# A hybrid decoder layer on one core: the mixer's units and attention heads put in another order, with roots, splits and constants done in other places

## What is computed

```
xn = rmsnorm(x, g_mix);  proj = xn @ w_in
q, k, v, u_pool, q_mem, gate_logits = split(proj)
q, k = rotary(rmsnorm(q, q_norm)), rotary(rmsnorm(k, k_norm))        # 8 heads, 2 maps of 64 each
o = (softmax(q1 k1) - lam * softmax(q2 k2)) @ v                      # causal, per head
y_attn = (rmsnorm(o, g_subln) * 0.8) @ w_b_attn
y_pool = multiscale_pool(u_pool) @ w_b_pool
y_mem  = softmax(rmsnorm(q_mem) rmsnorm(km) / sqrt(128)) @ vm @ w_b_mem   # km, vm = rmsnorm(mem) @ w_mem_kv
h = x + (g0*y_attn + g1*y_pool + g2*y_mem) @ w_out                   # g = sigmoid(gate_logits + b_gates)
out = h + moe(rmsnorm(h, g_ffn))                                     # top 4 of 32 experts, clamped SwiGLU
```

## Time and profile before

| | |
|---|---|
| median of 3 runs | 1288.76 us |
| the profiled execution, its own time | 1286.68 us |
| its span in the profile | 1284.8 us |
| granted TensorE clock, mean share of 2.4 GHz | 0.983 |
| TensorE busy | 1175.9 us, 92% of the span |
| VectorE busy | 464.6 us, 36% |
| ScalarE busy | 251.3 us, 20% |
| GpSimd busy | 20.8 us, 2% |
| DMA | 458.50 MB, mean 357 GB/s |

### The profile page before, as it was taken

The page is one execution under the profiler, slowest core; times in us unless marked ns, Lnnn a source line. Parts: engine busy times, 40 slices in busy tenths (PEclk is TensorE's granted clock), DMA queues, the critical chain, the costliest instruction groups (busy, mean ns, idle before and its releaser), DMA issues.

```text
span 1284.8 us, 13949 instructions
## 1 busy us (share of the span) xinstructions
PE 1175.9 (92%) x5444; PEld 590.3 (46%) x5444; DVE 464.6 (36%) x814; ACT 251.3 (20%) x378; POOL 20.8 (2%) x29
## 2 busy tenths in 40 slices
PE   6898999997889999999999999999999999999997
PEld 5686787775743343434344343434434333333332
DVE  6679878875441222122122222222121212212131
ACT  5444555542010010001001010100100010001100
POOL 0200000010000000000000000000000000000000
PEclk8998999998989999999999999999999999999999
DMA  8544355476679999999999999999999999999996
GB/s 284 204 133 162 131 206 173 146 264 251 245 293 425 396 389 430 427 429 428 429 428 429 428 429 428 429 428 429 428 429 428 429 428 428 428 428 428 428 428 287
DMA packets 59480, 458.50 MB, mean 357 GB/s; under 512 B 9216, under 2 KB 9856, under 8 KB 34880
## 3 DMA queue, kind: packets, MB, share of 16 engines
q1 hardware_dynamic: 57168, 454.18, 85.8%
q0 software_dynamic: 1104, 3.93, 0.9%
q10 hardware_dynamic: 1184, 0.07, 0.1%
HBM read 457.11 MB, written 1.05 MB: 357 GB/s over the span
## 4 chain that ended last, share of the span: by engine, by line
PE 68%; DMA 16%; DVE 10%; ACT 3%; issue 2%; DVEq 0%; ACTq 0%; SPq 0%
PE bank L1495 29%; DMA experts_ring<-in_w_down 14%; PE bank L1547 14%; PE bank L1253 12%; PE bank L1515 5%; PE bank L1483 3%; DVE ring_split L774 3%; PE bank L1501 2%; ACT region L744 1%; PE bank L1502 1%; PE bank L1222 1%; DMA small<-in_g_mix 1%; DMA ring<-in_w_in 1%; DVE region L1173 1%; ACT prob L649 1%
## 5 line engine op out<-in xcount | busy, mean ns | idle before, releaser
L1495 PE MATMUL bank<-experts_ring,region 128*64 128x512 f32 x2048 | 454.0, 596 | 11.5 <-DVE region L1182 6.6
L1495 PEld LDWEIGHTS bank<-experts_ring,region 128*64 128x64 f32 x2048 | 145.2, 137 | 291.6 <-issue 286.3
L1547 PE MATMUL bank<-experts_ring,region 128*64 128x512 f32 x1024 | 229.0, 596 | 31.8 <-ACT region L744 25.0
L1253 PE MATMUL bank<-ring_split,region_split 128*128 128x512 f32 x768 | 234.5, 407 | 21.2 <-DVE ring_split L774 11.3
L1253 PEld LDWEIGHTS bank<-ring_split,region_split 128*128 128x128 f32 x768 | 147.2, 195 | 56.0 <-DVE ring_split L774 13.0
L1547 PEld LDWEIGHTS bank<-experts_ring,region 128*64 128x64 f32 x1024 | 73.1, 137 | 167.1 <-issue 125.5
L1253 PE MATMUL bank<-ring_split 128*128 128x512 f32 x288 | 114.8, 399 | 0.0
L1207 DVE COPY region<-bank 64x512 f32<-64x512 f32 x32 | 22.2, 694 | 237.1 <-PE bank L1547 237.1
L1190 DVE TENSOR_SCALAR region<-bank 128x512 f32<-128x512 f32 x32 | 22.1, 692 | 209.7 <-PE bank L1502 209.7
L774 DVE TENSOR_TENSOR ring_split<-ring,ring_split 128x2048 fp32r<-128x2048 f32 x42 | 95.8, 2288 | 0.3
L529 ACT ACTIVATE ring_split<-ring 128x2048 fp32r<-128x2048 f32 x42 | 79.9, 1910 | 39.8 <-DMA ring<-in_w_out 16.8
(11 more groups left out here) (167 smaller groups left out, 616.3 us busy)
## 6 DMA issues: line engine op xcount, KB each, us to landing
experts_ring<-in_w_gate SPq DMA_DIRECT2D x64, 2048.0 KB, 26.2
experts_ring<-in_w_up SPq DMA_DIRECT2D x64, 2048.0 KB, 25.3
experts_ring<-in_w_down SPq DMA_DIRECT2D x64, 2048.0 KB, 28.2
ring<-in_w_in SPq DMA_DIRECT2D x28, 1024.0 KB, 5.2
ring<-in_w_mem_kv SPq DMA_DIRECT2D x4, 1024.0 KB, 8.9
ring<-in_w_b_attn SPq DMA_DIRECT2D x4, 1024.0 KB, 5.1
ring<-in_w_out SPq DMA_DIRECT2D x4, 1024.0 KB, 5.1
region<-in_b_gates POOLq DMA_DIRECT2D x6, 512.0 KB, 4.9
```

The source lines that it names most:

```text
L1253: ins = nc.tensor.matmul(UB[u % 3][:, :], a[:, k, toks], b[:, cols], start=(k == 0 and m == 0), stop=(k == k_n - 1 and m == 2))
L1495: ins = nc.tensor.matmul(dst[h * SLOTS:(h + 1) * SLOTS, :], XE[:, kk, e * SLOTS:(e + 1) * SLOTS], w[:, k, h * HALF:(h + 1) * HALF], start= ...
L1547: ins = nc.tensor.matmul(bank[2][h * SLOTS:(h + 1) * SLOTS, :], AHT[:, k, half * SLOTS:(half + 1) * SLOTS], w[:, k, h * HALF:(h + 1) * HAL ...
```

## The change

The order of the pieces becomes `pool, mk, q0, mv, q1, qm, k0, v0, k1, v1`, so that the q and k pieces, which are rotated, alternate with others. Piece 0 is multiplied as plain float32 from the raw halves, 8 matmuls a unit, with no split of halves 0 and 1. The mean square becomes a sum whose 1/n sits in the Square's scale, and every root is an addition and a power on GpSimd, `inverse_root`; ScalarE's square roots and VectorE's reciprocals are gone. The norms of q (attention) and q_mem are not applied to the rows: they go into the scale of the exponentials and into the factor of the maxima. Each head's output is squared, scaled, turned and split by itself (`o_squares`, `o_out`, `turn_o`, `oT`, `oT_lower`), inside the head loop. One table `SPLIT_AT` replaces the two: ScalarE and VectorE both do half 2n+3 with piece n's first unit and half 2n+4 with its second. The short vectors come packed, in three DMAs. The head loop's pass h now holds units 21+2h and 22+2h, and the copy of turned merged blocks no longer stands behind four upper halves.

```diff
-PIECES = ["pool", "mk", "mv", "qm", "q0", "q1", "k0", "k1", "v0", "v1", "gp0", "gp1", "wbp",
+PIECES = ["pool", "mk", "q0", "mv", "q1", "qm", "k0", "v0", "k1", "v1", "gp0", "gp1", "wbp",
...
-    for _at, _u, _H in ((UPPER_AT, _first, 2 * _n + 4), (UPPER_AT, _second, 2 * _n + 5),
-                        (LOWER_AT, _first, 2 * _n + 3), (LOWER_AT, _second, 2 * _n + 4)):
+    for _u, _H in ((_first, 2 * _n + 3), (_second, 2 * _n + 4)):
         if _H < 2 * len(PIECES):
-            _at[_u] = _H
+            SPLIT_AT[_u] = _H
...
+            def inverse_root(cols, eps, signal):
+
+                n_eps[0] += 1
+                nc.gpsimd.tensor_scalar(cols, cols, eps, None, ALU.add).then_inc(eps_added, 1)
+                pool.wait_ge(eps_added, n_eps[0])
+                nc.gpsimd.tensor_tensor(cols, cols, minus_half.to_broadcast([P, cols.shape[1]]), ALU.pow).then_inc(signal, 1)
...
+            def o_root(h):
+                pool.wait_ge(o_squared, 2 * h + 2)
+                inverse_root(stat[:, 128 + 2 * h:130 + 2 * h], EPS, o_scale_ready)
...
             for h in range(HEADS):
-                for_gate = [u for u in (22 + 2 * h, 23 + 2 * h) if UNITS[u][1][0] == "g"]
+                a, b = 21 + 2 * h, 22 + 2 * h
+                if h:
+                    o_squares(h - 1)
                 if h + 1 < HEADS:
                     exps(h + 1)
-                if h == HEADS - 1:
-                    aT(h)
-                if 22 + 2 * h in for_gate:
-                    gate_exp(22 + 2 * h)
-                if h < HEADS - 1:
-                    aT(h)
-                hi_at(22 + 2 * h)
+                if h:
+                    o_out(h - 1)
+                aT(h)
+                gate_exp_of(a)
                 if h + 2 < HEADS:
                     qkT(h + 2)
...
+                hi_after(a)
+                if h:
+                    oT(h - 1)
+                gate_exp_of(b)
+                hi_after(b)
...
-                group_root(u - 6, slice(col, col + 8), HD)
-                link(nc.vector.tensor_tensor(a, raw, stat[:, col:col + 8].unsqueeze(2).to_broadcast([P, 8, HD]), ALU.mult))
...
+                if w == 0:
+                    nc.vector.tensor_tensor(raw, a, b, ALU.add).then_inc(normed, 1)
+                else:
+                    link(nc.vector.tensor_tensor(raw, a, b, ALU.add))
+                    normed_by(u, raw, HD, 8, normed)
...
             for h in range(HEADS):
                 if h + 1 < HEADS:
                     head_max(h + 1)
-                unit(22 + 2 * h)
+                unit(21 + 2 * h)
                 if h + 1 < HEADS:
                     head_weights(h + 1)
-                    unit(23 + 2 * h)
...
+                if h:
+                    oT_lower(h - 1)
+                unit(22 + 2 * h)
             unit(37)
+            oT_lower(HEADS - 1)
...
+                    if H < EARLY:
+                        if k % 4 == 0:
+                            pe.wait_ge(raw_in[H], 16)
+                            pe.wait_ge(xT_copied, 2 * t + k // 4 + 1)
+                        ins = nc.tensor.matmul(UB[u % 3][:, :], XNT[2][:, k, toks], raw(H)[:, cols], start=(k == 0), stop=(k == k_n - 1))
...
             def values(h):
                 pe.wait_ge(at_copied, h + 1)
                 if h >= 1:
-                    pe.wait_ge(o_copied, h)
+                    pe.wait_ge(o_copied, 2 * h)
+                    pe.wait_ge(oT_split, h)
...
+                if h:
+                    turn_o(h - 1)
+                unit(22 + 2 * h)
+                values(h)
+            unit(37)
+            turn_o(HEADS - 1)
             unit(38)
             unit(39)
-            for j in range(4):
-                t, h = divmod(j, 2)
-                pe.wait_ge(o_normed, t + 1)
-                turn4(bank[3 + j], [O[:, t, (4 * h + b) * P:(4 * h + b + 1) * P] for b in range(4)], oT_done)
-            pe.wait_ge(oT_split, 2)
+            pe.wait_ge(oT_split, HEADS)
             unit(40)
```

More of the change, by code:

```diff
@@ L491, in _ @@
             gate_bias(2, "a", 0)
+            for h in range(3, HEADS):
+                o_root(h)
             pool.wait_ge(pv_done, HEADS)
-            root(2, slice(128, 144))
             nc.gpsimd.memset(OE, 0.0).then_inc(seed_clear, 1)
@@ L503, in _ @@
             pool.dma_start(WR, w_router.rearrange("(k p) e -> p k e", p=P)).then_inc(late_in, 16)
-            root(3, slice(4, 5))
-            root(4, slice(5, 6))
+            for t in range(NT):
+                pool.wait_ge(squares, 5 + t)
+                inverse_root(stat[:, 4 + t:5 + t], EPS, h_inv)
         @block.scalar
@@ L700, in _ @@
-            for u in range(40, 44):
-                hi_at(u)
-            for j in range(4):
+                hi_after(a)
[3 more added lines that the diff above has]
+                hi_after(b)
+            o_squares(HEADS - 1)
+            o_out(HEADS - 1)
+            gate_exp(37)
+            hi_after(37)
+            oT(HEADS - 1)
+            for u in (38, 39):
+                gate_exp(u)
+                hi_after(u)
+            hi_after(40)
+            hi_after(41)
@@ L820, in _ @@
+            dve.wait_ge(gain_in, 16)
+            for j in range(4):
+                x_turned(j)
+            lo_whole(2)
+            mem_turned(0)
+            mem_turned(1)
+            lo_after(0)
+            mem_turned(2)
+            mem_turned(3)
+            dve.wait_ge(unit_done, 2)
+            for j in range(4):
+                x_lower(j)
+            lo_after(1)
+            dve.wait_ge(vec_in, 16 * 2)
             lam4 = tmp[:, 1, 0:4 * HD].rearrange("p (a n) -> p a n", a=4)
@@ L1275, in _ @@
             pe.wait_ge(mT_copied, 4)
-            for u in range(3, 8):
-                unit(u)
+            unit(3)
+            pe.wait_ge(xT_split, 4)
+            unit(4)
+            unit(5)
+            pe.wait_ge(bank_read[1], 1)
             pe.wait_ge(band_in, 32)
@@ L1351, in turn_qk @@
                     pe.wait_ge(qkT_copied, h)
[L1352 removed]
+                turn4(bank[3], [part(t, h // 4)[:, (h % 4) * P:(h % 4 + 1) * P] for part in (q_part, k_part) for t in range(NT)], qk_done)
             def scores(h):
@@ L1566 @@
     arrays, args = {}, []
-    for name in _INS + ["table", "band"]:
-        a = {"table": table, "band": band}.get(name)
+    for name in _INS + ["table", "band", "vectors"]:
+        a = {"table": table, "band": band, "vectors": short_vectors(inputs)}.get(name)
         a = np.ascontiguousarray(inputs[name]) if a is None else a
```

635 lines of the change are left out of this document (327 added, 308 removed).

## The result

The changed kernel takes 1306.67 us (median of four runs, 1305.25 to 1307.64). The kernel before, timed beside it, takes 1289.01 us, so the ratio is 1.014, with a 95% interval from 1.0126 to 1.0154: **17.7 us slower**. The forecast was 12.7 us slower. The profiled execution of the changed kernel took 1307.0 us, 20.3 more than the 1286.68 of the one before.

A forecast was written before the change was run, and what follows sets the result against it. Bound up to the turn of h: TensorE's units, with VectorE and ScalarE between. The walk's +5.7, plus 4.0 for clock and 3.0 for GpSimd, gave +12.7: 1299.4 us profiled, 1301.5 median; range 1291.5 to 1310.5.

The forecast's parts named there:

- terms for the clock: Lower TensorE clock: 2.0 us behind the memory branch's wait, 2.0 in the short passes; bounds 0 and 8 together.
- Mark 1: First units, up to the end of unit 3: 37.3 us against 45.5 before, a gain of 8.2.
- Mark 2: End of unit 19 at 148.2 us, including a 5.9 us TensorE wait after unit 14, behind unit 13's rotation.
- The walk: Stepping through the engines' new order with profile prices up to the turn of h: +5.7 us before three extra costs.
- GpSimd term: Roots on GpSimd slowed by VectorE's rotations: 0.75 us for each of four k units, 3.0; bounds 0 and 8.
- rival that GpSimd is shut out during rotations: Roots get nothing while VectorE rotates: +5 on the forecast, 1306.5 us; chance 0.15.
- Mark 3: Heads, from unit 19 to the end of unit 39: 152.1 us, ending at 300.3 against 272.5 before.
- full pass: Head-loop pass with two halves to split: 18.2 us, where TensorE needs about 13.5.
- the circle: Head loop: ScalarE and VectorE handle the same half, so neither works while the other does; 18.2 us a turn.
- short pass: Head-loop pass whose second unit is short, with one half to split: 13.9 us, where TensorE needs 8 to 11.
- Mark 4: Units 40 to 46, starting where unit 39 ends: 41.3 us, ending at 341.6 against 335.2 before.
- faster: Rival: heads stay at TensorE's pace and the gap behind unit 39 goes, 1259.4 us; chance 0.05.

The follow-up runs named there:

- run 2: The kernel before with ScalarE's upper half no longer one half ahead from unit 20 on: 1308.51 us, ratio 1.016.
- run 1: The changed kernel with ScalarE's upper half again one half ahead from unit 20 on: 1273.02 us, ratio 0.9887.
- experiment 6: The changed kernel with 8 transposes of the identity before each head's turning and values, from head 1 on: 1305.28 us, ratio 1.0133.
- experiments 3 and 4: Changed kernel with scores ahead of values: 1298.88 us; with the turned output's upper copy first: 1310.16, and its lower half ahead of the weights too: 1299.39.
- experiment 8: Changed kernel with upper halves' lead from unit 14 and memory maxima ahead of unit 13's rotation: 1266.72 us; last version, scores ahead of values too: 1259.39.

## Why the prediction was right, and where its sizes were off

The sign, the place and the mechanism were right. The marks, in us from the start. The forecast's include its terms for the clock and GpSimd where they fall (5.0 up to unit 19, 2.0 in the heads):

```
                      before   forecast   measured
end of unit 3          45.5      37.3       36.0
end of unit 19           -      153.2      149.7
end of unit 39        272.5     307.3      314.7
turn of h             335.2     348.6      356.3
```

*Mark 1* was 1.3 too dear. The loads of the first weights landed sooner than in the kernel before: half 2's upper half starts at 16.64, not at 18.26, and all that follows hangs on it.

*Mark 2.* The walk without extras gave 148.2, and 149.66 came, 1.5 more; with mark 1's gain of 1.3 that makes 2.8 to account for. Its parts hold: the first maximum was forecast for 104.7 and came at 103.22, and the wait of TensorE was 5.9 and is 6.4. The 2.8 are that half microsecond, a wait of 1.0 in front of the turning of the memory branch's queries, and 1.25 for the clock, since the 12 products at 112.58 took 4.00 where 12 took 2.75 at full clock. I had allowed 2.0 for the clock there.

The *GpSimd term*, 3.0 with bounds 0 and 8, was at its lower end, and with it falls the rival that GpSimd is shut out during rotations. In the rotation of unit 12, GpSimd's rows

```profile
93.31 0.35 POOL L483 TENSOR_SCALAR stat<-stat 128x8 f32<-128x8 f32 x1 [4.54 <-DVE stat L900]
93.74 1.66 POOL L485 TENSOR_TENSOR stat<-stat,small 128x8 f32<-128x8 f32 x1
```

lie over VectorE's

```profile
93.80 0.69 DVE L928 TENSOR_TENSOR tmp<-region,rot 128x512 f32<-128x512 f32 x1
94.53 0.69 DVE L932 TENSOR_TENSOR region<-tmp 128x512 f32<-128x512 f32 x1
95.51 0.69 DVE L906 SCALAR_TENSOR_TENSOR region<-region,stat 128x512 f32<-128x512 f32 x1 [0.29 <-POOL stat L485]
```

VectorE waits 0.29 us for the root, and neither side is stretched. 2.0 for addition and power, the walk's own figure, was nearly right (93.31 to 95.40).

*Mark 3* is the step that was undersized: 152.1 by the walk from unit 19's end, 154.1 with the clock, and 165.0 measured. By its three parts: 48.1 up to the first `oT_lower` (47.3 forecast); 85.85 for the five passes (77.6); 31.1 behind them (27.2). The full pass was nearly right, 18.65 against 18.2: run 2 confirms the circle (17.2 in the kernel before) and run 1 dissolves it (12.7 to 14.5). The pass from 239.01 to 257.66 is the circle alone; in the one before it the chain also runs through a whole unit at the lower clock (7.09 us at 223.57), but VectorE waited only 0.4 us for it. **The term that failed is the short pass, 13.9 in the forecast and 16.33 measured** (in ScalarE's timeline the first exponentials of the two heads start at 204.01 and 220.34). The pieces in its chain above:

- Values and scores: 1.65 assumed, 3.33 measured (214.20 to the first maximum at 217.53), +1.7. I took them at full clock, and apart from the walk allowed 2.0 for the clock in all the short passes. In the pass TensorE stands for over 4 us, and the granted clock from 200 to 220 was 0.82. The five pieces in the chain above take 3.26 together, and at a clock of 1.00 they took 1.80 (experiment 6; 1.80 too in the last version of experiment 8). So 1.5 of the 1.7 is the clock, and in the three short passes it cost about 4 (the third has the five in 2.86), twice what I had allowed.
- The exponentials: 1.76 assumed, 2.15 measured. +0.4. The change lets them read their scale from a column of `stat` instead of holding a number, and each takes 0.49 and 0.59 where it took 0.40 and 0.49. The Trainium skill (ScalarE: Activation LUTs, What ACT_TABLE_LOAD costs) says that each per-partition pointer operand adds some 93 ns to an instruction. By that rule four exponentials a head cost 0.37 more, and the trace agrees (0.39). The forecast took the price of the old form.
- The lower half of the turned output up to the values (213.57 to 214.20): 0.35 assumed, 0.63 measured. +0.3.

This is 2.4 a short pass. The third, without `qkT`, was 2.0 over its 13.4, so the three make 6.9 of the 12.9 by which the walk's 152.1 fell short; 2.0 of the 12.9 had been allowed for the clock, which leaves 10.9. That the values and scores lie in the circle at all was in the walk and is right (experiments 3 and 4). Behind the last pass 3.9 were missing: again values at the low clock and 12 products in 4.60 instead of 2.75, and the turning of the eighth head, for which TensorE waited 1.1. There a GpSimd addition lay under a lower half and took 1.67 instead of 0.22.

*Mark 4* held: 41.3 forecast, 41.65 measured. Unit 40 follows without a gap. One statement in it was wrong: the load of w_out is on the chain again (322.77, 9.80). It costs little: between 314 and 357 TensorE waited 1.3 us in all, against the 1.2 that I had named. Behind the turn of h, -0.7 was forecast and the expert loop starts 20.3 later for a turn 21.1 later, which is -0.8.

The sum: -3.5 up to unit 19, +10.9 in the heads, +0.2 behind make 7.6 over the forecast of 12.7 in the profiled pair, or 20.3. That the total came no further out is in part luck: the 3.0 for GpSimd, which never came, covered as much of what the heads were short of. The medians lie 17.7 apart, as the profiled execution of before was under its median.

Of the rivals, "faster" named its condition rightly: 4.7 us of the two engines' work would have to overlap in a pass. The order of the changed kernel does not allow it. With the lead back it does, and then the change is faster. Its 1259.4 assumed heads at TensorE's pace with the rest unchanged; the lead alone gave 1273.0, and it took the maxima and the scores as well to come there.

What was not separated: which parts of the start (plain first piece, packed vectors, split loads) give the 9.5 us of mark 1; and, of the 15.1 us that the change is worth with the lead, which part of it gives how much.

## What to carry to other kernels

When two engines work on the same item one after the other, keep the first a whole item ahead in its queue. The engines' busy shares (20% and 34% here) don't show the loss; the sum of a pass along the chain, set against the third engine's need, does. Count that circle in the order that the change leaves, and price the third engine's short instructions in it at the clock that its own waiting will bring. And when a change that ought to help comes out slower, put back its orders one at a time: here all the rest of the change was worth 15 us, and one half's lead in a queue was worth 33.

## What the runs showed of the hardware

A GpSimd addition on two columns took 0.22 to 0.23 us where VectorE was idle, and 1.66 to 1.67 where a 2.29 us subtraction on VectorE had begun before it. In GpSimd's timeline of the changed kernel:

```profile
216.71 0.22 POOL L483 TENSOR_SCALAR stat<-stat 128x2 f32<-128x2 f32 x1 [15.31 <-ACT region L711]
...
253.36 1.67 POOL L483 TENSOR_SCALAR stat<-stat 128x2 f32<-128x2 f32 x1 [16.18 <-ACT region L711]
```

VectorE was idle for 2.89 us up to 217.53, and the lower half shown above ran from 252.65 to about 254.9: the long addition ends 0.1 behind it. But the power of 1.66 us at 93.74 did not hold up VectorE's multiplication at 93.80 and addition at 94.53, both with two operands in SBUF and begun while it ran; both kept their 0.69. The spans that the profile gives for GpSimd are rough, so this second reading is the less certain one; in all eight rotations of this kernel the power took 1.66 to 1.69. The Trainium skill (SBUF — State Buffer, SBUF: two separate sides) says that a VectorE instruction with two SBUF inputs and a GpSimd instruction that reads SBUF use a shared pair of ports, which whichever starts first holds for its whole instruction while the other is blocked. The first case is as that rule has it, the second is not.
